# A decoder layer's causal mask: VectorE's minimum in the score banks in place of products with the identity

## What is computed

```python
def block(args):                       # one block of 128 queries, j = 0..7
    q_blk, j = args
    s = jnp.einsum('bhcqd,bhckd->bhcqk', q_blk, k)      # c = 0, 1: two score matrices per head
    qpos = j * Q_BLOCK + jnp.arange(Q_BLOCK)
    mask = kpos[None, :] <= qpos[:, None]
    p = jax.nn.softmax(jnp.where(mask, s, -jnp.inf), axis=-1)
    a = p[:, :, 0] - lam * p[:, :, 1]
    return jnp.einsum('bhqk,bhkv->bhqv', a, v32)
...
g = jax.nn.sigmoid(gate_pre)
merged = g[:, :, 0] * ya + g[:, :, 1] * yb
h = h + jnp.einsum('bsd,de->bse', merged, w_out[l])
hn = rms_norm(h, norm_ffn_w[l])
u = jax.nn.relu(jnp.einsum('bsd,df->bsf', hn, w_ff1[l]))
h = h + jnp.einsum('bsf,fd->bsd', u * u, w_ff2[l])
```

## Time and profile before

| | |
|---|---|
| median of 3 runs | 1906.81 us (1903.93 to 1907.09) |
| profiled execution, its own time | 1905.65 us |
| span of its profile | 1903.7 us, 26951 instructions |
| PE busy | 1887.6 us (99%), 9960 products |
| weight loads (PEld) busy | 1618.5 us (85%) |
| VectorE busy | 1204.3 us (63%) |
| ScalarE busy | 948.4 us (50%) |
| GpSimd busy | 334.5 us (18%) |
| TensorE clock granted, mean | 0.998 of full |

### The profile page before, as it was taken

How to read it: one execution, slowest core, us unless ns; L and a number is a source line. 1 busy time by engine, 2 the same in 40 slices (tenths; PEclk the granted TensorE clock), 3 DMA queues, 4 the chain that set the end, 5 groups by cost and what they waited for, 6 DMA issues and landing times. The chain is left out here.

```text
span 1903.7 us, 26951 instructions
## 1 busy us (share of the span) xinstructions
PE 1887.6 (99%) x9960; PEld 1618.5 (85%) x9960; DVE 1204.3 (63%) x1560; ACT 948.4 (50%) x1541; POOL 334.5 (18%) x182
## 2 busy tenths in 40 slices
PE   9999999999999999999999999999999999999998
PEld 6989898989898989888888888878888888888887
DVE  7675758576767676644311122687778778789774
ACT  5455655556555655445333322237576585333343
POOL 2202020211111110232123444420000000121002
PEclk9999999999999999999999999999999999999999
DMA  5341515151424242432254444557677577454422
GB/s 213 112 155 67 177 56 193 51 197 50 175 66 151 87 159 83 165 106 72 75 191 150 140 141 171 179 182 265 206 258 274 200 277 234 184 224 147 147 83 89
DMA packets 103283, 292.86 MB, mean 154 GB/s; under 512 B 10889, under 2 KB 28041, under 8 KB 92193
## 3 DMA queue, kind: packets, MB, share of 16 engines
q1 hardware_dynamic: 100896, 283.36, 43.1%
q10 hardware_dynamic: 2304, 8.39, 1.1%
HBM read 204.61 MB, written 87.10 MB: 153 GB/s over the span
## 5 line engine op out<-in xcount | busy, mean ns | idle before, releaser
L753 PE MATMUL gp<-r1h,w_hi 128*128 128x512 f32 x880 | 346.7, 394 | 1.2 <-ACT ev L1146 1.2
L755 PE MATMUL gp<-r1h,w_lo 128*128 128x512 f32 x880 | 343.5, 390 | 0.0
L754 PE MATMUL gp<-r1l,w_hi 128*128 128x512 f32 x880 | 342.7, 389 | 0.0
L1034 PE MATMUL scores<-xh,qh 128*128 128x512 f32 x512 | 200.4, 391 | 3.0 <-ACT res L1417 2.1
L1038 PE MATMUL scores<-xh,ql 128*128 128x512 f32 x512 | 199.3, 389 | 0.0
L1036 PE MATMUL scores<-xl,qh 128*128 128x512 f32 x512 | 199.2, 389 | 0.0
L755 PEld LDWEIGHTS gp<-r1h,w_lo 128*128 128x128 f32 x880 | 165.2, 188 | 35.2
L753 PEld LDWEIGHTS gp<-r1h,w_hi 128*128 128x128 f32 x880 | 165.3, 188 | 34.3 <-issue 1.6
L754 PEld LDWEIGHTS gp<-r1l,w_hi 128*128 128x128 f32 x880 | 165.4, 188 | 32.2
L1263 ACT ACTIVATE pr<-scores,nb 128x256 f32<-128x256 f32 (+7 forms) x128 | 93.7, 737 | 117.1 <-DVE nb L1686 117.1
L2058 POOL TENSOR_TENSOR w_lo<-w_raw,w_hi 128x1024 fp32r<-128x1024 f32 x25 | 60.5, 2421 | 508.4 <-ACT w_hi L1137 486.2
(11 more groups left out here) (351 smaller groups left out, 4312.7 us busy)
## 6 DMA issues: line engine op xcount, KB each, us to landing
xraw<-xo_d SPq DMA_DIRECT2D x54, 1024.0 KB, 5.2
w_raw<-in_in_blocks SPq DMA_DIRECT2D x64, 512.0 KB, 3.7
proj_d<-ev SPq DMA_DIRECT2D x128, 256.0 KB, 2.2
rq<-in_ff_quarters SPq DMA_DIRECT2D x32, 1024.0 KB, 7.9
xo_d<-res SPq DMA_DIRECT2D x78, 256.0 KB, 3.2
xo_d<-ring SPq DMA_DIRECT2D x60, 256.0 KB, 3.0
gt<-proj_d SPq DMA_DIRECT2D x32, 256.0 KB, 3.3
xt<-in_x_halves SPq DMA_DIRECT2D x8, 512.0 KB, 7.2
```

Source lines behind the costliest of these rows:

```text
L753: pe.matmul(gp[half][:], wh[slot][:, k, :], mh[:, k, t], start=(k == 0), stop=False)
L754: pe.matmul(gp[half][:], wh[slot][:, k, :], ml[:, k, t], start=False, stop=False)
L755: mm = pe.matmul(gp[half][:], wl[slot][:, k, :], mh[:, k, t], start=False, stop=(k == KT - 1))
L1034: pe.matmul(bank, qh[s % 3][:, k, cols], xh[s % 3][:, k, :], start=first and k == 0, stop=False, skip_group_check=True)
```

## The change

The mask is applied by VectorE. The products with the identity are gone, 128 in all (8 heads, 8 blocks, 2 matrices). Before each row maximum VectorE now takes the minimum of the diagonal block of 128 columns, in place in the bank, with a constant of 128 columns that is -2^100 above the diagonal and 3e38 elsewhere. It is linked: VectorE waits for its end before the maximum reads the bank. The columns past the block are no longer masked; neither the maximum nor the exponential reads them. `mask` is loaded by its DMA as it is used; the rounded copy of the identity, the copy of the mask and a memset in the first round go.

In the last head's round ScalarE empties the third gate unit's bank in slot 0, behind the high parts of K, in place of slot 1.

In the feed-forward VectorE makes the weight sums 1, 2 and 3 of the next group in the stages idx = 4, 5 and 6, each behind that stage's low parts. Before, 1 and 2 stood in idx = 5 and 6 ahead of the low parts, and 3 stood in idx = 1 of the group itself, ahead of them. Only group 0 keeps its third sum in stage 1.

```diff
--- before.py
+++ after.py
@@ -189,9 +189,8 @@
         home["pair"] = nc.sbuf_base
         whp = sb("w_hi_pair", [P, KT, 2, P], F32R, heads)
         wlp = sb("w_lo_pair", [P, KT, 2, P], F32R, heads)
-        identr = sb("identr", [P, P], F32R, heads)
         keep = sb("keep", [P, P], F32, heads)
-        mask = sb("mask", [P, 3 * P], F32R, heads)
+        mask = sb("mask", [P, P], F32, heads)
         cosT = sb("cosT", [P, S], F32, heads)
         sinT = sb("sinT", [P, S], F32, heads)
         inv = sb("inv", [P, 1], F32, heads)
@@ -391,7 +390,7 @@
             "fq_ready", "fq_used", "f_sums_done", "f_ready", "f_std", "f_scaled"))
         ft_tr, ft_out, ft_act, out_st = sem("ft_tr"), sem("ft_out"), sem("ft_act"), [sem("out_st0"), sem("out_st1")]
 
-        DVE_HEAD = 47
+        DVE_HEAD = 63
 
         block = ctx.enter_context(nc.Block())
 
@@ -505,7 +504,7 @@
             wload_head(0, 1)
             sp.dma_start(cosT[:].bitcast(I32), positions[0].partition_broadcast(P)).then_inc(c2_in, 16)
             sp.dma_start(inv[:], c_inv).then_inc(c2_in, 16)
-            sp.dma_start(sg[:, 0:3 * P], c_mask).then_inc(c2_in, 16)
+            sp.dma_start(mask[:], c_mask).then_inc(c2_in, 16)
             sp.dma_start(keep[:], c_keep).then_inc(c2_in, 16)
             wload_head(0, 2)
 
@@ -864,17 +863,10 @@
 
                         width = (i + 1) * P if i % 4 == 2 else -(-(i + 1) // 2) * 2 * P
                         edges = [(0, width)] if width <= 512 else [(0, 512), (512, width)]
-                        m0 = width - 2 * P
-                        moff = 0 if width == (i + 1) * P else P
                         for c in range(2):
                             for lo, hi in edges:
-                                diag = lo <= m0 < hi
                                 q = qs[:, c, i * P:(i + 1) * P]
-                                if diag:
-
-                                    pe.matmul(sp_[:, c, m0:m0 + 2 * P], identr[:], mask[:, moff:moff + 2 * P],
-                                              start=True, stop=False, skip_group_check=True)
-                                pe.matmul(sp_[:, c, lo:hi], q, ka[:, c, lo:hi], start=not diag, stop=False,
+                                pe.matmul(sp_[:, c, lo:hi], q, ka[:, c, lo:hi], start=True, stop=False,
                                           skip_group_check=True)
                                 mm = pe.matmul(sp_[:, c, lo:hi], q, kb[:, c, lo:hi], start=False, stop=True,
                                                skip_group_check=True)
@@ -1329,8 +1321,14 @@
                     if k % 2 == 0 and s != 1:
                         split_hi(n + 1, (n + 1) // 2, (n + 1) % 2)
                 for k in GATE_UNITS_AT[s]:
-                    evac(N_GATE + k // 2, k % 2)
-                attend(NH - 1, s, lambda: None, None, lambda: split_hi(N_GATE + 2, (N_GATE + 2) // 2, 0))
+                    if k != 2:
+                        evac(N_GATE + k // 2, k % 2)
+
+                def third_unit():
+                    split_hi(N_GATE + 2, (N_GATE + 2) // 2, 0)
+                    evac(N_GATE + 1, 0)
+
+                attend(NH - 1, s, lambda: None, None, third_unit)
 
             def stage_hi(k):
                 act.wait_ge(x_in[k], X_LOADED[k] + 16)
@@ -1536,7 +1534,6 @@
 
             dve.memset(ckq[:, 0:CONV - 1], 0.0)
             dve.memset(qpad[DK:P, :], 0.0)
-            dve.memset(sg[:, 3 * P:], 0.0)
             dve.memset(cst[:], 0.0)
             pro.link(dve.memset(v1[:, :, DV:DV + 1], 1.0))
             pro.link(dve.memset(v1[:, :, DV + 1:VW], 0.0))
@@ -1574,8 +1571,6 @@
                 dve.tensor_scalar(tab[:], tab[:], -3.1415925, None, ALU.max).then_inc(pro_dve, 1)
 
             dve.wait_ge(c2_in, 16 * 4)
-            dve.tensor_copy(identr[:], ident[:])
-            pro.link(dve.tensor_copy(mask[:], sg[:, 0:3 * P]))
             pro.link(dve.tensor_copy(kqs[:], cosT[:].bitcast(I32)))
             pro.link(dve.tensor_scalar(ang, ang, inv[:, 0:1], None, ALU.mult))
             dve.wait_ge(c_in, 16 * 3)
@@ -1681,6 +1676,8 @@
                 if 0 <= i < TT:
                     for c in range(2):
                         dve.wait_ge(s_done, 2 * (TT * h + i) + c + 1)
+                        d = sp_[:, c, i * P:(i + 1) * P]
+                        chain.link(dve.tensor_tensor(d, d, mask[:], ALU.min))
                         m = dve.tensor_reduce(mx[:, c:c + 1], sp_[:, c, 0:(i + 1) * P], AX_X, ALU.max)
                     chain.link(m)
                     dve.tensor_scalar(nb[:], mx[:], -SCALE, None, ALU.mult).then_inc(nb_ready, 1)
@@ -2010,15 +2007,15 @@
                 else:
                     if 1 <= g <= GROUPS and idx == 1:
                         hidden_turned(g - 1, 3)
-                    if idx == 1:
-                        weight_sum(g, 3)
+                    if s == 1:
+                        weight_sum(0, 3)
                     if idx == 3 and g:
                         weight_sum(g, 4)
-                    if g < 2 * GROUPS - 1 and idx in (5, 6):
-                        weight_sum(g + 1, idx - 4)
                     if s + 2 < STAGES:
                         q_lo_part(s + 2)
                         x_lo_part(s + 2)
+                    if g < 2 * GROUPS - 1 and idx in (4, 5, 6):
+                        weight_sum(g + 1, idx - 3)
                     if 1 <= g <= GROUPS and idx == 0:
                         for u in range(3):
                             hidden_turned(g - 1, u)
@@ -2166,8 +2163,7 @@
     for base in (0, DK):
         col[base:base + 8, 0] = -inv
         col[base + 8:base + 16, 0] = inv
-    mask = np.zeros((P, 3 * P), np.float32)
-    mask[:, P:2 * P][np.arange(P)[None, :] > np.arange(P)[:, None]] = NEG
+    mask = np.where(np.arange(P)[None, :] > np.arange(P)[:, None], np.float32(NEG), np.float32(3e38))
     last = np.zeros((P, P), np.float32)
     last[P - 1, :] = 1.0
     carry = np.ones((NH, S), np.float32)
```

## The result

The changed kernel takes 1936.97 us (median of 4 runs, 1934.87 to 1937.50), the kernel before 1905.78: a ratio of 1.0163, 95% interval 1.0147 to 1.0179. The forecast was 1908.0 us, the range 1898 to 1916.

A forecast was written before the change was run, and what follows sets the result against it. PE, busy 99% of the span, was taken to bound the kernel: products -15.4, new waits +20.7, gate bank -1.4, weight sums -2.7, together +1.2 us, so 1908.0 us with the run offset; range 1898 to 1916.

The forecast's parts named there:

- What a minimum costs: VectorE in the attention: 0.29 us per minimum, 0.33 with its link, twice a slot, 0.66 us.
- Rival 1: Attention masks: writing the bank is dearer, 0.40 us per minimum, giving 1913.4 us; chance 0.20.
- rival 2: Attention masks: the link costs nothing, 0.20 us per minimum, giving 1898.6 us; chance 0.12.
- Rival 4: Attention: VectorE is idle for 37% of the span, so removed products are pure gain, 1887.3 us; chance 0.03.
- The waits that were forecast: Head rounds: new PE waits at blocks 1, 2, 3 and 7, 2.92 us a round, 20.7 us together.
- Block 5: no wait: Head rounds, block 5: `nb`, started 0.66 us later, still ends with the same GpSimd instruction, so PE loses nothing.
- the list of places where PE can wait: Attention slots: PE's room taken only from `a_done` or the last exponential to the first PE instruction needing it.
- The products taken away: PE in the attention: 128 products of 0.12 us removed, 15.4 us less, 0.24 us a slot.
- The weight sums: Feed-forward: with the third sum a group earlier, all four PE waits for ScalarE's copies go, 2.7 us less.
- The price is in idx = 5: Feed-forward: second sum ahead of the adds delays them, yet under 0.3 us remains before PE's products, covered narrowly.
- Rival 3: Feed-forward: the moved sums do not do their job, 2.7 us stay, giving 1910.7 us; chance 0.10.
- The gate bank: Last head's round: ScalarE empties the third gate unit's bank before PE needs it, 1.4 us less.

The follow-up runs named there:

- mask_alone: The changed kernel with its gate-bank and weight-sum parts undone, so only the masks by minimum differ from the kernel before; 1926.26 us.
- sums_alone: The kernel before with only the change's weight-sum part, the sums behind the low parts; 1919.07 us.
- gate_alone: The kernel before with only the change's gate-bank part, the copy behind K's high parts; 1903.86 us.
- sums_order: The kernel before with weight sums 1 and 2 moved behind the low parts in stages 5 and 6, sum 3 left in stage 1; 1930.80 us.
- mixed_masks: The kernel before, mask products replaced only in block 4 and the last round by one VectorE addition over both banks; 1909.21 us.
- conv_later: The kernel before with masks by one minimum over both banks, and the gate's convolution and its dependent steps one slot later; 1936.26 us.
- gate_sums: The kernel before with the gate bank's copy behind K and all three weight sums ahead of the low parts in stages 4 to 6; 1901.16 us.

## Why the prediction was wrong, by its steps

- **What a minimum costs**: right. 0.290 us forecast and measured, in 128 instructions, 0.33 with its link. Rival 1 (0.40 for writing a bank) and rival 2 (no price for the link, 0.20) are both refuted, and with the first the estimate of 0.065 us more, taken from the Trainium skill's page Perfetto Trace Analysis, section Optimizing Scalar/DVE Operations. Rival 4 fails by the sign.
- **The waits that were forecast** come out, a little smaller. The forecast counted them from start to start; so counted, mask_alone has in its fourth round 1.46 us at block 1 (1.71 forecast), 0.33 and 0.50 at blocks 2 and 3 (0.35 and 0.56), 0.26 behind block 7's exponentials (0.30): 2.55 us against 2.92.
- **The step that failed first: "Block 5: no wait", and with it the list of places where PE can wait.** Behind block 5 it costs 0.74 us. Block 5 was missed because I moved VectorE's start and left GpSimd's where it was. In slot 10, behind the scores of block 7, PE waits for the last low part `atl` of block 5, 0.62 us; the prediction looked only at `a_done` and the exponentials. Two more steps are 0.21 and 0.15 us too long (block 1's scores to the next product, and behind the scores of block 6), 0.3 are in the first `ka` products, which take over the longer first step behind transposes that the mask's product took before, and some 0.6 in the steps that follow the waits. In all, PE's row in that round gains 5.2 us beside the product steps, against 2.92 forecast. That less 2.13 us of products is the 3.09 measured; forecast was 2.92 - 1.92 = 1.0. In seven rounds the step is off by 14.6 us.
- **The named waits agree by chance.** The profile names 20.1 us of new waits in the rounds, and 20.7 were forecast. But the one leaves out some 0.16 us for each wait and holds two kinds that the forecast did not have, and the other has the full cost of those that it knew. What is to be held against 20.7 is some 36, seven times 5.2.
- **The products taken away**: their own steps were right (2.13 us a round measured, 1.92 forecast), the booking was not. I added a saving to waits worked out apart. The experiments give 9.1 us without minimums and 0.9 with them.
- **The weight sums**: -2.7 us forecast, +10.7 measured in the profile of the changed kernel, +13.8 in the runs of sums_alone. The step that failed is "The price is in idx = 5", with its "covered, narrowly": I asked only whether PE would find its next bank free. It does. But the adds also release ScalarE's squares, these `turned`, that its stores, and those the copies of the next group, 33 us later. Rival 3 named this move and gave it 2.7 us of lost gain as its worst, so the range's upper end knew nothing of it.
- **The gate bank**: -1.4 forecast; the wait is gone in every kernel with it, and gate_alone's interval (0.2 to 3.8 us faster) holds the forecast.

Of the miss of 29 us half (14.6) lies in the rounds, about 13.4 us in the sums (10.7 + 2.7), and 1.3 at the start, which scatters from kernel to kernel.

## What to carry to other kernels

A cost moved from a full engine to one with room at its side is hidden only if every path through the new place has room, that of third engines too (here ScalarE's `w_hi` and the GpSimd instruction that `nb` ends with); where one has not, the saving is not subtracted from the wait, it disappears in it. Put filler work where its engine waits anyway, ahead of the instruction that waits: the same three sums gained 4 us there and lost 14 behind it. For a moved step ask who is released by what it delays, to the end of the chain, not only whether the next instruction on the bound engine still finds its buffer.

## What the runs showed of the hardware, unexpected

- **TensorE's clock falls behind a wait**, and that can cost nearly as much as the wait. Granted 1.00 before, 0.51 in the 6.3 us after the 3.12 us wait at 1404, steps 0.43 us instead of 0.227. The wait's length alone does not say it. In the feed-forward the clock fell behind waits of 5.37, 4.56, 4.51 and 4.46 us (all four of sums_order), 3.12 (the changed kernel), 2.80 and 2.51 (sums_alone) and 1.81 (mixed_masks), and not behind 2.95 and 2.48 (sums_alone) nor 2.39, 2.37 and 2.16 (the changed kernel); in the rounds of conv_later it fell behind each of the four waits of 2.6 to 2.7. Which of the shorter waits is punished stays open. It is a likely reason why sums_alone ran 2.3 us further above the kernel before in its runs (13.8) than in its profile (11.3): its two longest runs (1920.2 us) have a mean clock of 0.995, the profiled one (1917.0) 0.997; but that was not tried.
- **VectorE and GpSimd hold each other up**: `qraw` took 3.43 us beside `w_lo` in four rounds of conv_later, 1.22 elsewhere; in the other three `w_lo` took 4.27 us where the four have 3.1. A bias of two columns (`nb`) took 1.06 us in the changed kernel where 0.17 is usual, and ended with GpSimd's instruction.
- **A minimum in place in a score bank** takes VectorE 0.290 us for 128 columns, as much as a sum from a bank into SBUF, and 0.425 for 256 columns over two banks.
- **The start scatters.** The first scores of the attention come between 116.7 and 118.8 us in these profiles, in kernels that hardly differ up to there; the granted clock from 10 to 20 us was 0.83 in the kernel before and 0.66 in the changed one, and 1.00 in gate_sums, whose first scores come at 116.9. Of the 31.5 us between the two spans 1.3 are this.
